# Mixer 1's head steps and attention in closer, later steps, a convolution tap on ScalarE, and smaller edits in mixer 2 and at the end

## Chip, core and metric

One core of a Trainium2 chip runs the whole program. The metric is the device time of one execution in microseconds, the median of several; lower is better.

## What is computed

A batch of one, 256 tokens, 1024 channels, all in float32. Two blocks follow each other. The part that matters here is the first block's hybrid mixer and what lies around it:

```python
proj = h @ w_in                      # c_q, c_kv, k_rope, conv_in (3 x 512), gate_logits (2 x 1024)
q = rms_norm(c_q) @ w_uq             # 8 heads, 64 + 32 (rope)
kv = rms_norm(c_kv) @ w_ukv          # 8 heads, 64 + 64
# q and k: rms norm per head, rope on the 32; causal softmax attention -> o_attn
u = gate_c * xv
u = conv1d(u, conv_w, kernel=3, causal, per channel)
o_conv = gate_b * u
merged = sum(sigmoid(gate_logits) * (branches @ w_branch))
y = merged @ w_out
```

Before it stands a SwiGLU FFN (width 2816), behind it another; the second block has two attentions (A: 8 heads of 128, B: dilated groups with a bias), gates, an MLP of 4096, a gated embedding, and a last RMS norm over the 1024 channels of each token, whose result is stored.

## The kernel before

Activations lie channels by tokens. Weights stream from HBM in units of 128 x 2048 float32 (1 MB; 16 tiles of 128 x 128), in the order of `unit_list`, into four raw buffers. ScalarE casts each unit to a rounded high part (`hi`, two halves of 1024 columns), VectorE makes the low part, raw minus high (`lo`, per half), into a ring of four. A tile is then three matmuls, high by high, high by low and low by high, over 256 token columns or 258: the last two hold the modulation's shift through the same weights, which is read out of the bank as one column. `ada` units in the same stream are the modulation's matrices; VectorE reduces them against silu(c).

`Plan` writes one list of steps; each engine's program runs its own steps of the list in that order, so the list fixes every queue. A counter of tiles paces the work beside the matmuls: `need` takes units up to three ahead, `fill` and every fourth tile (`PACE`) emit one pending piece (an `ada` or a `lo` half) where more than two are pending, `in_tiles` runs a function so many tiles later, and a side generator is advanced each time that the tile count passes a multiple of `every`.

Mixer 1, after the query and key products, counts tiles from 0: conv_out 0 is 0 to 16, conv_in 2 to 32, conv_in 3 to 48, conv_out 2 to 64, then eight blocks of gates to 192 (order 1, 2, 0, 3 to 7). Each block has two banks of a ring of four, freed when both VectorE's product with the token factor (`rbc`) and ScalarE's copy of the shift column are through. `heads(t)` (`heads_q`, `heads_rope`; VectorE) norms and rotates the queries of 128 tokens at tiles 17 and 20. `head_keys` (`heads_k` on VectorE, `heads_kr` on ScalarE) is at tile 34. The attention starts at tile 42, a step at each multiple of `STEP_1` = 7 of the whole count: eight head turns (four for queries, four for keys; TensorE transposes, ScalarE copies out), then eleven steps of `in_steps`. In step n these emit `normal_1(n-1)`, `scores_1(n)` with `masked_1` and `exp_1`, `turn_1(n-2)` with its copy `turned_1`, and `pv_1` of the pair that ends with n-3 with `o_hi_1`, `o_lo_1`. The first turn falls on tile 54, the first scores on tile 110, the last step on tile 180. The turned probabilities have one bank, the scores two.

`conv` (VectorE) takes conv_in's two products to u, then three taps: one tensor_scalar and two scalar_tensor_tensor. `gate_tanh` follows this chain for each half of a gates block: ScalarE's `gate_shift`, VectorE's `gate_in`, which waits for the shift, a halving of the shift by ScalarE, the tanh.

In mixer 2 attention B has steps of `STEP_B` = 12 tiles beside the 128 tiles of gate_a and out_a; what is left is emitted behind them at once (`finish_side`). At the end the second token half's result is scaled by ScalarE (columns 0 to 511) and VectorE (512 to 1023) and stored in one transfer of 512 KB.

## Time and profile before

| | us |
|---|---|
| median of 3 runs | 1015.24 (1014.84 to 1017.86) |
| the profiled execution | 1014.84 |
| its span, first to last instruction | 1013.1 |
| TensorE busy | 983.3 |
| VectorE busy | 776.2 |
| ScalarE busy | 536.2 |

By stage the span divides into a start to 18 us, the first FFN to about 217, mixer 1 to about 385, the second FFN to 594, mixer 2 to 765, the MLP to about 975 and the end. A timeline row is start, length, engine, line, operation, out<-in, count, and in brackets the idle time before it and what ended it. Helpers record all operations, so lines say little and tiles (sb_ring are weights, sb_tq and sb_tmp temporaries, sb_zb the shift columns, sb_junk<-sb_raw an ada piece, R the big shared region) say more. PEclk is the granted TensorE clock, 1.00 for the higher of its two levels.

### The profile page before, as it was taken

The numbers are of one execution on the slowest core, as the hardware profiler recorded it, in microseconds if no ns is written. First come the engines' busy times: TensorE is split into PE (matmuls) and PEld (weight loads), VectorE is DVE, ScalarE is ACT, GpSimd is POOL, SyncE is SP. The second block draws the span as 40 slices with busy tenths as digits, with TensorE's granted clock in tenths as the row PEclk, the third lists the DMA queues.
The fourth block names the chain that finished last, engine by engine and source line by source line (L and its number), as shares of the span: only waits on it lengthen the run. The fifth ranks groups of instructions, "written<-read, shape, count | busy, mean of one in ns | idle before, by whom it ended". The sixth has DMA issues, their size and how long they took to land.

```text
span 1013.1 us, 17325 instructions
## 1 busy us (share of the span) xinstructions
PE 983.3 (97%) x7016; PEld 917.8 (91%) x7016; DVE 776.2 (77%) x1423; ACT 536.2 (53%) x937; POOL 12.5 (1%) x32
## 2 busy tenths in 40 slices
PE   5999999999898999999999999999999999999996
PEld 4999998999897999999998988789999988988895
DVE  6999998979976887685776588556778877577665
ACT  5455554436576555453555545664555655355453
POOL 0000000004000000000000000000000000000000
PEclk9999999999999999999999999999999999999999
DMA  8996999855572655678664535364454555555531
GB/s 334 352 345 268 350 344 341 298 205 209 177 276 93 213 200 174 240 240 209 246 241 174 191 135 208 125 182 136 141 186 168 196 173 203 196 178 173 181 105 41
DMA packets 33277, 213.92 MB, mean 211 GB/s; under 512 B 3757, under 2 KB 6189, under 8 KB 8494
## 3 DMA queue, kind: packets, MB, share of 16 engines
q1 hardware_dynamic: 32910, 211.78, 59.5%
q8 instruction: 55, 0.90, 0.3%
q10 hardware_dynamic: 288, 1.05, 0.3%
q14 instruction: 24, 0.20, 0.1%
HBM read 210.19 MB, written 2.62 MB: 210 GB/s over the span
## 4 chain that ended last, share of the span: by engine, by line
PE 89%; DVE 6%; ACT 3%; issue 1%; DMA 1%; DVEq 0%; ACTq 0%
PE bank L216 87%; PE bank L219 2%; DVE sb_ring L195 1%; ACT sb_tmp L192 1%; ACT sb_ring L192 1%; ACT R L192 1%; DVE sb_tq L195 1%; DVE sb_tmp L195 1%; DVE sb_junk L204 1%; DMA sb_raw<-wts 0%; DMA sb_x<-xt 0%; DVE sb_acc L195 0%; DVE sb_st_v L207 0%; DVE sb_tmp L198 0%; DVE sb_nst L195 0%
## 5 line engine op out<-in xcount | busy, mean ns | idle before, releaser
L216 PE MATMUL bank<-sb_h,sb_ring 128*128 128x258 f32 (+2 forms) x3776 | 496.4, 292 | 6.7 <-DVE sb_h L201 3.9
L216 PEld LDWEIGHTS bank<-sb_h,sb_ring 128*128 128x128 f32 x3776 | 475.7, 190 | 20.9 <-issue 5.7
L195 DVE TENSOR_TENSOR sb_ring<-sb_raw,sb_ring 128x1024 fp32r<-128x1024 f32 (+1 forms) x324 | 385.2, 1205 | 2.8 <-ACT sb_ring L192 2.8
L192 ACT ACTIVATE sb_ring<-sb_raw 128x1024 fp32r<-128x1024 f32 (+1 forms) x324 | 320.4, 1038 | 79.3 <-DMA sb_raw<-wts 47.1
L216 PE MATMUL bank<-R_512r,sb_ring 128*128 128x256 f32 (+1 forms) x1608 | 225.3, 301 | 0.0
L216 PEld LDWEIGHTS bank<-R_512r,sb_ring 128*128 128x128 f32 x1608 | 211.3, 188 | 11.9 <-issue 0.3
L216 PE MATMUL bank<-sb_ring,sb_h 128*128 128x512 f32 (+1 forms) x504 | 112.5, 378 | 0.0
L216 PEld LDWEIGHTS bank<-sb_ring,sb_h 128*128 128x128 f32 x504 | 87.4, 188 | 16.6
L204 DVE CUSTOM_DVE_ANT_0 sb_junk<-sb_raw,sb_csil,sb_cols 128x1024 bf16<-128x1024 f32 x72 | 92.3, 1282 | 1.8
L216 PE MATMUL bank<-R_1024r,sb_ring 128*128 128x512 f32 (+1 forms) x576 | 91.6, 320 | 0.0
L216 PEld LDWEIGHTS bank<-R_1024r,sb_ring 128*128 128x128 f32 x576 | 82.0, 188 | 8.2
L195 DVE TENSOR_TENSOR sb_tq<-bank,sb_rbc 128x256 f32<-128x256 f32 x87 | 34.6, 421 | 62.5 <-ACT sb_zb L192 40.3
L192 ACT ACTIVATE R_512r<-sb_tq 128x256 fp32r<-128x256 f32 x60 | 25.2, 420 | 77.1 <-DVE sb_tq L195 50.1
L192 ACT ACTIVATE sb_tmp<-bank 128x256 f32<-128x256 f32 (+2 forms) x62 | 27.9, 462 | 30.0 <-PE bank L216 27.7
L192 ACT ACTIVATE sb_tmp<-sb_tmp,sb_smx 128x256 f32<-128x256 f32 (+2 forms) x40 | 21.0, 526 | 34.8 <-DVE sb_smx L204 24.5
L201 DVE SCALAR_TENSOR_TENSOR sb_x<-bank,sb_gcol,sb_x 128x256 f32<-128x256 f32 x36 | 17.4, 482 | 27.5 <-PE bank L216 27.1
L192 ACT ACTIVATE sb_h<-sb_x,sb_cols 128x256 fp32r<-128x256 f32 x24 | 14.2, 592 | 37.5 <-DVE sb_x L201 24.0
L195 DVE TENSOR_TENSOR R_512r<-sb_tq,R_512r 128x256 fp32r<-128x256 f32 x60 | 25.2, 420 | 3.9 <-ACT R_512r L192 3.9
L192 ACT ACTIVATE sb_tq<-bank 128x256 f32<-128x256 f32 (+1 forms) x35 | 12.9, 368 | 27.1 <-PE bank L216 27.0
L195 DVE TENSOR_TENSOR sb_tmp<-bank,sb_tmp 128x256 f32<-128x256 f32 x32 | 12.4, 425 | 19.0 <-ACT sb_tmp L192 19.0
L219 PE MATMUL bank<-sb_con,sb_tmp 128*128 128x128 f32 (+1 forms) x134 | 21.2, 276 | 6.0 <-ACT sb_tmp L192 4.2
L192 ACT ACTIVATE sb_tq<-sb_tq,sb_zb 128x256 f32<-128x256 f32 x26 | 13.3, 511 | 23.7 <-DVE sb_tq L195 23.6
(158 smaller groups left out, 558.1 us busy)
## 6 DMA issues: line engine op xcount, KB each, us to landing
sb_raw<-wts SPq DMA_DIRECT2D x193, 1024.0 KB, 4.9
sb_raw<-wts SPq DMA_DIRECT2D x3, 512.0 KB, 3.9
scratch<-R SPq DMA_DIRECT2D x1, 1536.0 KB
sb_x<-xt ACTq DMA_DIRECT2D x2, 512.0 KB, 5.2
out<-R SPq DMA_DIRECT2D x2, 512.0 KB, 2.6
R<-scratch SPq DMA_DIRECT2D x2, 508.0 KB, 8.9
sb_raw<-wts SPq DMA_DIRECT2D x1, 768.0 KB, 4.5
sb_raw<-wts SPq DMA_DIRECT2D x1, 640.0 KB, 4.0
```

What stands on the lines that cost most here:

```text
L192: return Issued(self.e and self.e.activation(o, i, func, **kw))
L195: return Issued(self.e and self.e.tensor_tensor(*a))
L201: return Issued(self.e and self.e.scalar_tensor_tensor(*a))
L204: return Issued(self.e and self.e.tensor_tensor_reduce(*a))
L216: return Issued(self.e and self.e.matmul(o, w, m, start=start, stop=stop, skip_group_check=True))
L219: return Issued(self.e and self.e.transpose(o, i, ident))
```

## The change

Times of steps in mixer 1: `HEADS_AT` (17, 20) to (37, 53), `KEYS_AT` 34 to 75, `ATTENTION_AT` 42 to 70, and the generator is advanced each 3.5 tiles instead of 7. A head turn takes one such half step; a step of the attention takes two (`in_half_steps`): scores, turn and pv in the first, the norm of the scores just made and the copy-out of the last pv in the second. By the tile count the turns fall on tiles 75, 79, 82, 86 (queries), 89, 93, 96, 100 (keys), the scores on 103, 110 and so on, their norms on 107, 114 and so on, the last first-half step on 173.

While that generator's stretch lasts (`apart`), the cast of a unit is emitted in two places: its first half when the unit is taken, its second just ahead of the unit's first `lo`.

In the convolution the tap of a token itself is one ScalarE pass (`conv_tap`), between `conv_u` and the other two taps, with one more `fill` there. In gates, VectorE's `gate_in` of both halves comes first and waits for the matmuls alone; ScalarE's `gate_shift` halves in the same pass and frees the bank; the separate halving is gone. `exp_ready` is a one-element exp after the first FFN's up blocks. `STEP_B` is 10.5. The last result is scaled in quarters of 256 columns and stored as two transfers (each two runs of 256 columns per token).

```diff
-STEP_1, STEP_A, STEP_B = 7, 11, 12
-HEADS_AT, KEYS_AT, ATTENTION_AT = (17, 20), 34, 42
+STEP_1, STEP_A, STEP_B = 7, 11, 10.5
+HEADS_AT, KEYS_AT, ATTENTION_AT = (37, 53), 75, 70
...
-            self.add("hi", i, w)
+            self.add("hi", i, w, (0,) if self.apart else (0, 1))
+            if self.apart:
+                self.late.add(w)
...
+            if name == "lo" and a[0] in self.late:
+                self.late.remove(a[0])
+                self.add("hi", i, a[0], (1,))
             self.add(name, i, *a)
...
+        self.add("exp_ready")
         self.add("gcol", 0, 0.5)
...
             self.fill()
-            self.add("conv", i, xs, zc, y)
+            self.add("conv_u", i, xs, zc, y)
+            self.add("conv_tap", i, y)
+            self.fill()
+            self.add("conv", i, y)
...
             banks = project(("gates", f), [128, 128], between)
+            qs = [tq.take() for _ in banks]
             for i, b in enumerate(banks):
-                zb, q = m.zb.take(), tq.take()
+                self.add("gate_in", f, i, b, qs[i])
+            for i, b in enumerate(banks):
+                zb, q = m.zb.take(), qs[i]
                 self.add("gate_shift", f, i, b, zb)
-                self.add("gate_in", f, i, b, q)
-                done(b, ("gate_in", f, i))
+                done(b, ("gate_shift", f, i))
                 self.add("gate_tanh", f, i, q, zb)
...
-                    self.add("o_hi_1", h // 2, o)
+                    o_b.append((h // 2, o))
+
+            def between(n):
+                if n < 8:
+                    self.add("normal_1", n, p_b[n])
+                if o_b:
+                    hp, o = o_b.pop()
+                    self.add("o_hi_1", hp, o)
                     self.fill()
-                    self.add("o_lo_1", h // 2, o)
-                    done(o, ("o_1", h // 2))
-
-            yield from in_steps(scores, lambda h: self.add("normal_1", h, p_b[h]), turn, pv)
+                    self.add("o_lo_1", hp, o)
+                    done(o, ("o_1", hp))
+
+            o_b = []
+            yield from in_half_steps(scores, turn, pv, between)
 
         def start():
-            self.side, self.every = attention(), STEP_1
+            self.side, self.every, self.apart = attention(), STEP_1 / 2, True
...
         self.finish_side()
+        self.apart = False
...
         self.add("final_factor", 1)
-        self.add("final", 1)
-        self.add("store", 1)
+        for half in range(2):
+            self.add("last_final", half)
+            self.add("last_store", half)
...
+def in_half_steps(scores, turn, pv, between):
+
+    for n in range(11):
+        yield
+        for i, stage in ((0, scores), (2, turn), (3, pv)):
+            if 0 <= n - i < 8:
+                stage(n - i)
+        yield
+        between(n)
...
+        e.dma_start(quarters(m.out[1, :, :], half), quarters(m.result(1), half)).then_inc(
+            *self.up(f"out{1 + half}_out", ("out", 1 + half), by=16))
...
+    def conv_tap(self, i, y):
+
+        e = self.e
+        e.wait_ge(*self.at("conv_u", i))
+        e.wait_ge(*self.at("cols"))
+        e.activation(y.ap[:, 0:T], y.ap[:, T:2 * T], scale=self.m.cc("conv", 8 + i)).then_inc(
+            *self.up("conv_tap", ("conv_tap", i)))
...
+        e.activation(m.smx[0:1, 0, 7:8], m.ones[0:1, 0:1], FN.Exp).then_inc(*self.up("scalar_own"))
...
-        e.wait_ge(*self.at("project", ("gates", f)))
-        e.activation(zb.ap[:, 0:1], bank.ap[:, T:T + 1]).then_inc(*self.up("shift_out", ("gate_shift", f, i)))
+        e.wait_ge(*self.at("gate_in", f, i))
+        e.activation(zb.ap[:, 0:1], bank.ap[:, T:T + 1], scale=0.5).then_inc(*self.up("shift_out", ("gate_shift", f, i)))
...
-        e.activation(zb.ap[:, 1:2], zb.ap[:, 0:1], scale=0.5).then_inc(*self.up("scalar_own"))
-        e.wait_ge(*self.last())
-        e.wait_ge(*self.at("gate_in", f, i))
...
-        e.wait_ge(*self.at("gate_shift", f, i))
+        e.wait_ge(*self.at("project", ("gates", f)))
         e.tensor_tensor(q.ap, bank.ap[:, 0:T], m.rbc, ALU.mult).then_inc(*self.up("gate_in", ("gate_in", f, i)))
```

## Rows read from the trace of the kernel before

**Rows 1.** The page's first part and two of its costliest groups (busy, instructions; mean ns)
```profile
PE 983.3 (97%) x7016; PEld 917.8 (91%) x7016; DVE 776.2 (77%) x1423; ACT 536.2 (53%) x937; POOL 12.5 (1%) x32
...
L195 DVE TENSOR_TENSOR sb_ring<-sb_raw,sb_ring 128x1024 fp32r<-128x1024 f32 (+1 forms) x324 | 385.2, 1205 | 2.8 <-ACT sb_ring L192 2.8
L192 ACT ACTIVATE sb_ring<-sb_raw 128x1024 fp32r<-128x1024 f32 (+1 forms) x324 | 320.4, 1038 | 79.3 <-DMA sb_raw<-wts 47.1
```

**Rows 2.** Windows by stage: length, busy us (count) by engine, PEclk, DMA, GB/s
```profile
240.00:262.00 22.00, 19.42 (x152) 18.63 (x150) 21.41 (x53) 11.03 (x20) 7.41 (x19) 1.00 0.55 192
262.00:285.00 23.00, 22.83 (x176) 22.50 (x177) 22.02 (x36) 16.01 (x33) 0.00 (x0) 0.93 0.58 194
285.00:330.00 45.00, 39.85 (x315) 36.99 (x314) 30.54 (x87) 30.91 (x85) 0.00 (x0) 1.00 0.45 165
```

**Rows 3.** The same view in steps of 10 us, the one with a lower clock
```profile
260.00:270.00 10.00, 7.83 (x51) 7.65 (x52) 9.79 (x20) 5.31 (x12) 0.00 (x0) 0.83 0.23 67
```

**Rows 4.** TensorE's timeline in mixer 1: start, us, instructions, idle before
```profile
254.15 5.67 PE L216 MATMUL bank<-sb_h,sb_ring 128*128 128x258 f32 x45 [0.40 <-ACT sb_zb L192]
262.17 4.12 PE L216 MATMUL bank<-sb_h,sb_ring 128*128 128x258 f32 x18 [2.35 <-ACT sb_zb L192]
266.13 0.60 PE L219 MATMUL bank<-sb_con,R 128*96 128x128 f32 x4
...
269.11 0.60 PE L219 MATMUL bank<-sb_con,R 128*96 128x128 f32 x4
...
298.42 0.55 PE L219 MATMUL bank<-sb_con,sb_tmp 128*128 128x128 f32 x3 [1.20 <-DVE sb_tmp L198]
...
308.37 0.55 PE L219 MATMUL bank<-sb_con,sb_tmp 128*128 128x128 f32 x3 [1.81 <-ACT sb_tmp L192]
```

**Rows 5.** VectorE's timeline in mixer 1, forms apart
```profile
237.08 0.35 DVE L198 TENSOR_SCALAR sb_tmp<-sb_tmp,sb_cols 128x256 f32<-128x256 f32 x1
...
256.83 0.69 DVE L195 TENSOR_TENSOR R<-R,sb_st_z 128x512 f32<-128x512 f32 x1
...
261.43 0.42 DVE L195 TENSOR_TENSOR sb_tq<-bank,sb_rbc 128x256 f32<-128x256 f32 x1
...
265.05 1.29 DVE L195 TENSOR_TENSOR R<-R,sb_st_z 128x512 f32<-128x512 f32 x2
...
270.10 1.00 DVE L201 SCALAR_TENSOR_TENSOR sb_tmp<-sb_tmp,sb_cols 128x255 f32<-128x255 f32 x2
...
279.08 0.42 DVE L195 TENSOR_TENSOR sb_tq<-bank,sb_rbc 128x256 f32<-128x256 f32 x1
```

**Rows 6.** ScalarE's timeline, end of the first FFN and mixer 1
```profile
148.80 2.01 ACT L192 ACTIVATE sb_ring<-sb_raw 128x1024 fp32r<-128x1024 f32 x2 [0.85 <-DMA sb_raw<-wts]
...
262.15 0.51 ACT L192 ACTIVATE sb_tq<-sb_tq,sb_zb 128x256 f32<-128x256 f32 x1
...
292.52 1.28 ACT L192 ACT_TABLE_LOAD   x1 [2.35 <-DVE sb_smx L204]
...
294.89 0.20 ACT L192 ACTIVATE sb_zb<-sb_zb 128x1 f32<-128x1 f32 x1
```

**Rows 7.** TensorE's timeline, end of attention B
```profile
739.74 0.60 PE L219 MATMUL bank<-sb_con,sb_tmp 128*128 128x128 f32 x4
741.52 1.09 PE L216 MATMUL bank<-sb_tmp,R 128*64 128x128 f32 x16 [1.18 <-ACT sb_tmp L192]
```

**Rows 8.** SyncE's timeline before attention B
```profile
683.58 1.24 SPq L222 DMA_DIRECT2D R<-scratch  x2
```

**Rows 9.** DMA issues by line: KB each, median us to landing
```profile
out<-R SPq DMA_DIRECT2D x2, 512.0 KB, 2.6
...
R<-scratch SPq DMA_DIRECT2D x2, 258.0 KB, 5.6
```

**Rows 10.** Timeline of the last 17 us, VectorE's last instruction
```profile
1009.15 0.75 DVE L201 SCALAR_TENSOR_TENSOR R<-R,sb_nst,R 128x512 f32<-128x512 f32 x1
```

**Rows 11.** Windows at the end
```profile
1011.00:1011.50 0.50, 0.00 (x0) 0.00 (x0) 0.00 (x0) 0.00 (x0) 0.00 (x0) 0.50 0.99 410
```

More of the change, by code:

```diff
@@ L425, in p_pair, with quarters @@
         return self.reg(34, 512, F32R), self.reg(36, 512, F32R)
+def quarters(ap, half):
+    return ap.rearrange("p (a s n) -> p a s n", a=2, s=2)[:, :, half, :]
 def by_head(ap):
@@ L473, in __init__ @@
         self.pend, self.split, self.hold = [], set(), False
+        self.apart, self.late = False, set()
         self.tiles, self.side, self.every, self.later = 0, None, 4, []
@@ L1330, in run @@
                  "bias_store": self.bias_store, "load_bias": self.load_bias, "load_p": self.load_p,
-                 "store": self.store, "end": self.end}
+                 "store": self.store, "last_store": self.last_store, "end": self.end}
         for name, args in self.plan.steps:
@@ L1410, in load_p, with store, last_store @@
             *self.up("gain_in", ("fin_row",), by=16))
-    def store(self, i):
+    def store(self):
         m, e = self.m, self.e
-        e.wait_ge(*self.at("final_low", i))
-        if i:
-            e.wait_ge(*self.at("final_high", i))
-        e.dma_start(m.out[i, :, :], m.result(i)).then_inc(*self.up(f"out{i}_out", ("out", i), by=16))
+        e.wait_ge(*self.at("final"))
+        e.dma_start(m.out[0, :, :], m.result(0)).then_inc(*self.up("out0_out", ("out", 0), by=16))
+    def last_store(self, half):
+        m, e = self.m, self.e
+        e.wait_ge(*self.at("final_low", half))
+        e.wait_ge(*self.at("final_high", half))
+        e.dma_start(quarters(m.out[1, :, :], half), quarters(m.result(1), half)).then_inc(
+            *self.up(f"out{1 + half}_out", ("out", 1 + half), by=16))
     def end(self):
         e = self.e
-        e.wait_ge(*self.at("out", 0))
-        e.wait_ge(*self.at("out", 1))
+        for i in range(3):
+            e.wait_ge(*self.at("out", i))
         e.wait_ge(*self.at("scratch"))
@@ L1906, in run, with hi @@
                 steps[name](*args)
-    def hi(self, i, w):
+    def hi(self, i, w, parts):
         m, e = self.m, self.e
@@ L1912, in hi @@
             e.wait_ge(*self.at("used", w - NS))
-        for p in range(2):
+        for p in parts:
             a, b = m.half(w, p)
@@ L2629, in conv_c, with conv_u @@
         e.tensor_tensor(y.ap[:, T:2 * T], bank.ap[:, 0:T], m.rbc, ALU.mult).then_inc(*self.up("conv_c", ("conv_c", i)))
-    def conv(self, i, xs, zc, y):
-        m, e = self.m, self.e
-        u, yy = y.ap[:, T:2 * T], y.ap[:, 0:T]
-        w = [m.cc("conv", 4 * n + i) for n in range(3)]
+    def conv_u(self, i, xs, zc, y):
+        e = self.e
+        u = y.ap[:, T:2 * T]
         e.wait_ge(*self.at("conv_xs", i))
@@ L2638, in conv @@
             *self.up("conv_u", ("conv_u", i)))
-        e.wait_ge(*self.last())
-        self.ts(yy, u, w[2], ALU.mult)
+    def conv(self, i, y):
+        m, e = self.m, self.e
+        u, yy = y.ap[:, T:2 * T], y.ap[:, 0:T]
+        w = [m.cc("conv", 4 * n + i) for n in range(2)]
+        e.wait_ge(*self.at("conv_tap", i))
         for n in (1, 2):
-            e.wait_ge(*self.last())
+            if n == 2:
+                e.wait_ge(*self.last())
             e.scalar_tensor_tensor(yy[:, n:T], u[:, 0:T - n], w[2 - n], yy[:, n:T], ALU.mult, ALU.add).then_inc(
```

52 lines of the change are left out of this document (29 added, 23 removed).

## Prediction

> **What bounds the kernel now.** I read the page's first part, then the windows of the three engines by stage, then TensorE's timeline in every stretch that is not full, and for each gap there the timelines of VectorE and ScalarE. TensorE is busy 983.3 us of a span of 1013.1 [rows 1]. It starts late and ends early by about 20 us together; the gaps between hold under 10 us. They lie where the change works. From 240 to 262 us TensorE misses 2.58 us while VectorE is busy 21.41 of 22; from 262 to 285 VectorE is still busy 22.02 of 23 and TensorE nearly full; from 285 to 330 TensorE misses 5.15 us while no engine is full [rows 2]. So the first is a VectorE backlog, the last a chain of short waits. One gap costs twice: between 260 and 270 the granted clock is 0.83 of full [rows 3], which is 3.4 us at the lower level (1.2 GHz) and 1.7 us of matmul work lost, right behind the longest wait of the mixer, 2.35 us. The matmuls show it: 18 of them take 4.12 us there [rows 4], where the prices below give 2.2. In mixer 2, TensorE waits 1.18 us in the last step of attention B, which falls behind the tiles that should cover it [rows 7].
>
> Prices I use throughout: seven tiles (21 matmuls) and one head turn repeat every 2.98 us (266.13 to 269.11) [rows 4]; I split this as 0.365 us a tile and 0.42 a turn, which also fits 45 matmuls in 5.67 us [rows 4].
>
> **Part 1, heads and keys later.** The 2.35 us wait is for a bank that conv_in 2 holds; its VectorE product runs at 261.43, and just ahead of it stand both heads' query steps, 256.83 to 261.43, 4.60 us [rows 5]. TensorE had conv_in 2 behind it just before 254.15 [rows 4], so VectorE lagged by 8 us. Moved to tiles 37 and 53, the heads leave that place. The four tensor_scalar taps also leave VectorE, 0.35 us each, 0.39 with the gap to the next [rows 5]; two of them (0.78 us) stand before this point. So conv_in 2 is read at 261.43 - 4.60 - 0.78 = 256.05, and TensorE wants the bank at 259.4: the 2.35 us go, and the 1.7 us of slow clock with them. The 0.40 us wait at 254.15 [rows 4] hangs on a shift copy behind VectorE's convolution gate, which comes 0.78 earlier: it goes too. Gain 0.40 + 2.35 + 1.70 = 4.45 us.
>
> The work is moved, not removed, so I follow VectorE's queue. In the plan the extra fill in each conv_in takes one weight half (1.2 us [rows 1]) earlier and the pacing then takes one fewer: counting pending halves block by block gives the same number ahead of every tile multiple of 16. heads(0) then ends near 262.8; conv_in 3 is read by 263.5, wanted at 265.2 (tile 64 is 259.4 + 16 x 0.365). heads(1), before the gates of conv_out 2, ends at 271.0 (end of conv_in 3's convolution in before, 270.10 + 1.00 [rows 5]) less the 1.2 of heads_k (row at 265.05), less 1.56 for four taps, plus 1.13 for the weight half now ahead of it: 269.4. The first query turn is at tile 75, TensorE's 269.3. **New wait 0.1 to 0.3.** heads_k, at tile 75, comes behind everything that stood before gates 1's first product at 279.08 [rows 5], less four taps: done at 277.5. The first key turn is at tile 89: 269.3 + 0.2 + 14 x 0.365 + 4 x 0.42 = 276.3. **New wait 1.2 us**, bounds 0 (a weight half slips behind it) and 2.6 (one more slips ahead; the clock stays up, as it did through 1.81 us [rows 2, 4]). I take 1.5 for both. Behind the waiting turn TensorE holds the tiles of gates 0; VectorE and ScalarE gain on it meanwhile. Banks: gates 1's are free near 278.7, wanted at 281: covered.
>
> The taps on ScalarE: the nearest row is a 128x256 pass with a per-partition operand, 0.51 us [rows 6]. ScalarE must wait for conv_u first, with a cast queued behind it (up to 1.6 us later for conv_in 2). In the trace the halves that VectorE takes next were cast some 4 us before; nothing reaches TensorE. Bounds 0 and 0.5; I take 0.
>
> **Part 2, first attention, 5.15 us of gaps.** Three causes show. (a) The first exp loads its table, 1.28 us at 292.52 [rows 6], with VectorE's next product behind it; the first gap, 1.20 us before turn(0) at 298.42 [rows 4], follows. exp_ready puts the load behind the first FFN's last silu, where ScalarE idles 0.85 us for a transfer until 148.80 [rows 6]: the load delays that cast by some 0.45 us, for weights that are three units away. Cost 0; with the cover gone it would be 1.28 on a cast that still has that lead. The tanh of the gates run behind this exp without another load, so it holds. (b) In each gates block VectorE's product waits for ScalarE's shift, and ScalarE passes a second tiny copy (0.20 [rows 6]): two round trips of 1.2 us in order. Now VectorE reads at once, and ScalarE has two shifts and two tanh without a wait between the engines: some 1 us less on it per block. (c) A weight cast holds ScalarE for 2.0 us in one piece, two halves of 1.04 [rows 1]; 1.81 us of gap at 308.37 [rows 4] end on a copy out of the turn bank that stood behind casts. Apart, it blocks 1.04. Besides, normal(n) comes three tiles (1.1 us) earlier against turn(n). The start is one step earlier (scores at tile 103 instead of 110), the period of seven tiles stays, and the last step is at tile 173 of 192. The window from 285 to 330 holds some ten steps: (45 - 5.15)/10 = 3.98 us of TensorE each, and 3.1 of ScalarE and 3.05 of VectorE [rows 2]. At 78% on both, in an order that alternates between them, some waits stay. Gain between 3.0 and 5.15; I take 5.15 - 0.6, plus 0.3 for six restarts of the array, whose first group takes longer (estimated at 0.05 each): 4.85 us.
>
> **Part 3, second attention.** Steps of 12 tiles start at tile 12 of 128; the eleventh lands behind tile 128, where turn(7) (739.74) and the product that waits for its copy stand together [rows 7]. In steps of 10.5 it lands at tile 125. Gain 1.2. It starts 4 tiles (1.5 us) earlier, near 690; the bias rows it needs are issued at 683.58 and 684.4 [rows 8] and such a transfer lands after 5.6 us [rows 9], at 690: at worst VectorE waits 0.5 there, with one weight half behind it. Bounds 0.6 and 1.2; I take 1.2.
>
> **Part 4, the end.** The last 512-column operation of VectorE (0.75 us from 1009.15 [rows 10]; ScalarE has its like beside it) becomes two of about 0.45 (256 columns take 0.42 [rows 5]), so the first half's store is issued 0.3 us earlier, the second at the old time with half the bytes. The old store lands 2.6 us after issue [rows 9], of which 512 KB at the 410 GB/s of its own time [rows 11] are 1.25. Half the bytes: 0.6 less at most, but both halves share the engines and rows of 1 KB are less efficient. Bounds -0.5 and +0.4; I take -0.2. The Trainium skill speaks on both sides here ("Perfetto Trace Analysis", DMA Optimizations): pieces under 2 KB carry "significant per-transfer overhead", and splitting lets some start sooner when the engines are idle. "DMA: Bandwidth & Descriptors" (its fit under the two cost components) has 2.0 us plus bytes at 436 GB/s, by which the last piece would end 0.6 us sooner, an estimate; the trace has 2.6 for 512 KB where the fit gives 3.2, so it already disagrees by as much.
>
> **Sum**, against the profiled execution (1014.84 us, 1.7 outside its span): -4.45 + 1.5 - 4.85 - 1.2 - 0.2 = -9.2, so 1005.6. The median run lies 0.4 above the profiled one: **1006.0 us**.
>
> **Rivals.**
> A, the debt comes back: heads and keys are now so late that turns wait longer than 2 us and the clock falls again as it did at 262. Price: waits of 3 instead of 1.5, and 1.7 for the clock: +3.2, 1009.2. For it: VectorE is busy 22.02 of 23 there, and my margins are 1 to 2 us. Against: moved items keep their place among known neighbours, and a shorter gap of 1.81 us left the clock alone.
> B, the attention is bound by the single turn bank and ScalarE's load of 78%: only 2.5 of 5.15 go. +2.4, 1008.4.
> C, all waits go and no new one comes: -1.5 and -0.6 more, 1003.9.
> D, slower: the second half of each cast now stands in ScalarE's queue just ahead of its lo piece, behind exps that wait for VectorE; VectorE then waits in order and TensorE runs out of weights. Seven units are taken while apart is on. It decides from 9.2/7 = 1.3 us of stall a unit; at 2 us a unit it is +4.8 net, 1020. Against: about 4 us between cast and use in the trace, and three units of lead.
> E, the early load does not help because a load stands at the first exp anyway: +1.2, 1007.2, inside the main range.
>
> **How the numbers follow.** Forecast with E 0.60, A 0.15, B 0.13, C 0.09, D 0.03. The range 1002.8 to 1010.0 takes in A, B, C and the bounds (new waits 0 to 3, attention 3.0 to 5.15, end -0.5 to +0.4). About 0.3% (3 us) is what a measurement of this kernel can tell from no change; faster by more: the forecast, B, C and nearly all of A, 0.92; same 0.05; slower 0.03.
>
> **What would show it.** Right: no 2.35 us gap ahead of conv_out 2 and granted clock 1.00 through 260 to 300; heads_k ending within 1 us of the first key turn, with a short gap there; no table load between 280 and 300, one near 148; under 1 us of gaps in the attention; no gap at attention B's last product. Wrong: a slow-clock stretch near 270 to 280 (A); gaps ahead of turn groups at each cast (B); TensorE waiting for VectorE's sb_ring (D).

## The result

The changed kernel takes 1011.21 us (median of 5 runs, 1010.49 to 1012.35), the kernel before 1017.16 beside it (5 runs, 1014.84 to 1017.98): ratio 0.9948, 95% interval 0.9937 to 0.9959. It is faster by about half a per cent. Forecast were 1006.0 us and a range that ends at 1010.0, so the time lies above the range; faster by over 0.3% (0.92) held. The two profiled executions, 1014.84 and 1011.21 (span 1009.4), differ by 3.6 us where the working had 9.2.

Page after (busy time of the engines; the group of VectorE's weight pieces), to be read with [rows 1]. TensorE's work is the same, and VectorE's pieces now wait 10.3 us for ScalarE's casts instead of 2.8:

```profile
PE 982.6 (97%) x7016; PEld 917.6 (91%) x7016; DVE 774.3 (77%) x1420; ACT 535.0 (53%) x927; POOL 11.8 (1%) x32
...
L195 DVE TENSOR_TENSOR sb_ring<-sb_raw,sb_ring 128x1024 fp32r<-128x1024 f32 (+1 forms) x324 | 385.6, 1205 | 10.4 <-ACT sb_ring L192 10.3
```

Windows after (busy of PE, PEld, DVE, ACT, POOL, then PEclk), to be read with [rows 2, 3]:

```profile
240.00:262.00 22.00, 22.00 (x175) 21.48 (x174) 21.11 (x48) 14.83 (x26) 7.47 (x22) 1.00 0.55 197
...
262.00:285.00 23.00, 19.89 (x154) 19.37 (x154) 21.26 (x40) 12.58 (x25) 0.00 (x0) 0.93 0.60 217
...
285.00:330.00 45.00, 43.35 (x348) 40.51 (x347) 32.37 (x90) 28.95 (x77) 0.00 (x0) 1.00 0.46 165
...
270.00:280.00 10.00, 7.02 (x45) 6.79 (x46) 9.96 (x18) 6.12 (x15) 0.00 (x0) 0.83 0.57 206
```

The first window is full now, but the second lost what it gained: TensorE misses 3.11 us there, and the granted clock of 0.83 moved from 260 to 270 into 270 to 280. The attention misses 1.65 instead of 5.15. TensorE's timeline after, every row of mixer 1 with a new or changed gap, then the start of the branch matmuls and the gate group behind attention B ([rows 4, 7] before):

```profile
235.53 6.79 PE L216 MATMUL bank<-sb_ring,R_512r 128*128 128x512 f32 x34 [1.12 <-ACT sb_tq L192]
...
270.03 0.53 PE L219 MATMUL bank<-sb_con,R 128*96 128x128 f32 x3 [0.15 <-DVE R L195]
...
276.48 1.09 PE L219 MATMUL bank<-sb_con,R 128*96 128x128 f32 x4 [2.96 <-ACT R L192]
...
299.21 0.55 PE L219 MATMUL bank<-sb_con,sb_tmp 128*128 128x128 f32 x3 [0.26 <-ACT sb_tmp L192]
...
319.85 0.55 PE L219 MATMUL bank<-sb_con,sb_tmp 128*128 128x128 f32 x3 [1.39 <-ACT sb_tmp L192]
...
334.46 5.80 PE L216 MATMUL bank<-R_512r,sb_ring 128*128 128x256 f32 x47
...
738.74 3.02 PE L216 MATMUL bank<-sb_h,sb_ring 128*128 128x256 f32 x24
```

The ledger against the kernel before, from the starts of like groups in both timelines (the branch is the first of the branch matmuls behind mixer 1's gates): queries 234.49 to 235.53, **1.04 late**; branch 337.71 to 334.46, **3.25 early**; the first group of the next ada unit 574.49 to 571.78, **2.71 early**, so 0.54 is given back in the second FFN; last scaling operation 1009.15 to 1005.25, **3.90 early** (1.2 from attention B); from there to the end 3.95 before and 4.15 after. Sum 3.7.

### The profile page after: what moved, and what is told of

The parts are those of the page before. It is cut to its first block, busy times and chain, and to the rows that moved or that the text cites. A ratio compares the mean times of both kernels' runs of the same rounds, so it can differ in the third digit from the quotient of the medians.

```text
span 1009.4 us, 17305 instructions
## 1 busy us (share of the span) xinstructions
PE 982.6 (97%) x7016; PEld 917.6 (91%) x7016; DVE 774.3 (77%) x1420; ACT 535.0 (53%) x927; POOL 11.8 (1%) x32
## 3 DMA queue, kind: packets, MB, share of 16 engines
q10 hardware_dynamic: 288, 1.05, 0.3%
HBM read 210.19 MB, written 2.62 MB: 211 GB/s over the span
## 4 chain that ended last, share of the span: by engine, by line
PE 80%; DVE 9%; ACT 4%; DMA 4%; issue 2%; SPq 0%; DVEq 0%; ACTq 0%
PE bank L216 78%; DMA sb_raw<-wts 3%; DVE sb_ring L195 2%; ACT sb_ring L192 2%; PE bank L219 2%; ACT sb_tmp L192 1%; DVE sb_junk L204 1%; DVE sb_tq L195 1%; DVE sb_tmp L195 1%; DMA R<-rows 1%; DVE sb_tmp L201 1%; ACT R L192 0%; DMA sb_x<-xt 0%; DVE R_512r L195 0%; DVE sb_tmp L198 0%
## 5 line engine op out<-in xcount | busy, mean ns | idle before, releaser
L195 DVE TENSOR_TENSOR sb_ring<-sb_raw,sb_ring 128x1024 fp32r<-128x1024 f32 (+1 forms) x324 | 385.6, 1205 | 10.4 <-ACT sb_ring L192 10.3
```

Source lines behind the costliest of these rows:

```text
L195: return Issued(self.e and self.e.tensor_tensor(*a))
```

## The experiments

Times are of one profiled execution each, but for the last version's; the kernel before took 1014.95, 1016.49, 1016.53, 1017.04 and 1016.21 beside the five sets. Diffs are against the changed kernel. Executions of one kernel differ by up to 4 us (1007.38 to 1011.39 for the last version), so the argument rests on starts within the traces, not on these times. A single start is not exact either: the two small transposes at 231 us, ahead of what the edits change in mixer 1, start between 230.9 and 231.3 (where the ada unit isn't moved). The time between two events of one trace is free of that.

Three events come back below. The product is VectorE's first pass on the banks of conv_out 0, near 252 us. The turn is the first head turn that waits for VectorE, near 270. The branch is the start of the branch matmuls, near 334.

### The tap by ScalarE

```diff
-self.add("conv_tap", i, y)      # ScalarE
+self.add("conv_tap_v", i, y)    # VectorE, the tensor_scalar of before
```

> The changed kernel with the token's own tap of all four conv_in blocks back on VectorE, in the same place of the order and with the same fills. Theory Q (the tap holds ScalarE's queue: its cast and the copy c_sums_out behind it free the bank that the query products want): the 1.12 us wait of TensorE before the query products (235.5 us) is gone, they start within 0.1 us of the kernel before (234.5), and VectorE's waits of 0.24, 0.17 and 0.47 us between 234 and 241 go too. VectorE then carries 4 x 0.39 us more, so its convolution gate of conv_out 2 comes about 0.7 later than in the changed kernel while TensorE is 1.0 earlier: the wait at the third query turn grows from 2.96 to about 4.7. Rival (the wait before the queries comes from the extra fill, not from the tap): it stays at 1.0 or more.

1011.45. The 1.12 us gap is gone, and the queries start at 234.30. So the tap has a cost where the prediction put none. ScalarE's timeline after shows how:

```profile
232.76 0.51 ACT L192 ACTIVATE sb_tmp<-sb_tmp,sb_cols 128x256 f32<-128x256 f32 x1 [0.63 <-DVE sb_tmp L201]
233.17 1.99 ACT L192 ACTIVATE sb_ring<-sb_raw 128x1024 fp32r<-128x1024 f32 x2
235.07 0.21 ACT L192 ACTIVATE sb_tq<-bank 128x72 f32<-128x72 f32 x1
```

The tap waits 0.63 us for `conv_u`; the cast (2.0 us, 232.12 before) starts 1.05 late, and behind it stands the 0.21 us copy that frees the bank TensorE wants for the queries. But the time did not fall: the gap at the first waiting head turn grew from 0.15 to 1.16 us (270.41), and one of 1.35 came at 281.81. The branch starts at 334.83. The third turn waits 2.95 us as in the changed kernel, where 4.7 was expected, and this time no stretch of half clock follows.

### Moving head steps and the attention's start

```diff
-HEADS_AT, KEYS_AT, ATTENTION_AT = (37, 53), 75, 70
+HEADS_AT, KEYS_AT, ATTENTION_AT = (17, 20), 34, 70    # heads as before
```

> The changed kernel with heads and keys back at tiles 17, 20 and 34; the attention still starts at tile 70 in half steps. Theory D (the heads' 4.6 us of VectorE set when conv_in 2's banks come free): a wait of about 2 us before conv_out 2 returns near 260 us, with 3.4 us of the lower clock behind it. Theory S (the wait at the third query turn is ScalarE's queue held by VectorE's lag, whatever the heads are): the lag is paid at conv_out 2, heads_kr is out of ScalarE's way (0.7), and the wait at the third turn falls from 2.96 to under 1 us. Rival (the heads only have to be done before their turns, VectorE's total does not matter): no wait returns at conv_out 2, and the one at the turn goes; the kernel would be 4 us faster than the changed one.

1011.6. The waits at the first and third turn and the slow stretch behind them are gone; in their place TensorE waits 2.05 us at 262.12, with 3.4 us of half clock behind it, and 1.19 at 281.85:

```profile
262.12 11.72 PE L216 MATMUL bank<-sb_h,sb_ring 128*128 128x258 f32 x81 [2.05 <-ACT sb_zb L192]
```

The branch is at 334.93. **The later heads alone bring 0.5 us at the branch**, where the prediction had 2.55 (2.35 and 1.7 gained, 1.5 lost). Starting the attention 7 or 14 tiles later (`ATTENTION_AT` 77, 84):

> The changed kernel with the attention's start at tile 77 instead of 70: first turn on tile 82, third on 89, scores from 110 as in the kernel before, last step 180. Theory S (ScalarE's copy of the first turn stands behind a whole cast and conv_hi, which wait for VectorE; it ends at 277): TensorE reaches the third turn about 2.9 us later, so the wait of 2.96 us shrinks to under 0.8 and the clock stays at its higher level; the start of the branch products comes 3 to 4.5 us earlier. The whole cast at tile 64 is still whole, and one more at tile 80 is split. Rival (the key turns would wait next, for heads_k, which ends at 278.0): a new wait of 1 us or more at tile 96.

1013.93; the third turn's gap grows to 5.75 us, where under 0.8 was expected.

> The changed kernel with the attention's start at tile 84: first turn on tile 89, scores from 117, last step 187 of 192. Theory S: no wait of over 0.3 us at any turn, clock full from 20 us to the end of the last gates; like the start at 77 or up to 0.8 us better there. Rival (the end of the attention then stands too close to the branch products): the last norms, turns and the copy-out of the last pair end behind tile 192, and TensorE waits at the first branch block, 1 us or more.

1013.81; 4.18 us, where no wait was expected. The branch is at 337.6 both times. The tile count does not decide how long the third turn waits: in both kernels, ScalarE's copies of the first turns stand behind gate steps that wait for VectorE.

### Four banks for the head turns

```diff
+four = [B[0], B[3], B[1], B[7]]
-b = A[hp % 2].take()
+b = four[hp % 4].take()
```

> The changed kernel with the head turns over four PSUM banks instead of two, so that the third turn has a bank without waiting for ScalarE's copy of the first. Theory V: VectorE is the bound, so TensorE runs on by one or two blocks and pays elsewhere: at the first key turn (tile 89), which needs heads_k, done at 278.0 in the changed kernel and wanted at about 276, 1 to 2 us, or at the bank of gates 0; the sum of waits between 260 and 290 stays above 2 us, but as no single wait is over 2.5 the clock may stay up. Theory B2 (the two turn banks are the cause): no wait over 0.5 us between 260 and 290, branch products 4.5 us earlier.

1011.36. The 2.96 us wait is gone, so its cause was the turn bank, which ScalarE read out late. In the changed kernel ScalarE's copies (275.76) stand behind a cast and conv_hi (272.93), and conv_hi waits for VectorE, which is late. VectorE's timeline after has `conv_gated`:

```profile
272.42 0.48 DVE L201 SCALAR_TENSOR_TENSOR sb_tmp<-sb_tmp,sb_zb 128x256 f32<-128x256 f32 x1
```

and ScalarE's timeline of the same kernel:

```profile
272.93 0.42 ACT L192 ACTIVATE R_512r<-sb_tmp 128x256 fp32r<-128x256 f32 x1 [1.39 <-DVE sb_tmp L201]
273.26 1.99 ACT L192 ACTIVATE sb_ring<-sb_raw 128x1024 fp32r<-128x1024 f32 x2
275.15 0.71 ACT L192 ACTIVATE R<-sb_tq 128x256 f32<-128x256 f32 x2
275.76 1.24 ACT L192 ACTIVATE R<-bank,sb_wqk 96x512 f32<-96x512 f32 x2
```

Yet the branch comes later, at 335.18. TensorE now reaches what lies behind sooner, and waits there, by its timeline in this kernel:

```profile
277.70 0.29 PE L219 MATMUL bank<-sb_con,R 128*96 128x128 f32 x1 [0.70 <-ACT R L192]
...
283.11 0.64 PE L219 MATMUL bank<-sb_con,R 128*96 128x128 f32 x4 [1.35 <-ACT R L192]
...
299.42 0.90 PE L219 MATMUL bank<-sb_con,sb_tmp 128*128 128x128 f32 x3 [2.19 <-ACT sb_tmp L192]
```

and ScalarE's timeline of the same kernel:

```profile
281.43 1.06 ACT L192 ACTIVATE sb_ring<-sb_raw 128x1024 fp32r<-128x1024 f32 x1 [1.49 <-DMA sb_raw<-wts]
```

The 1.35 us are a wait for a copy behind this cast, which waits 1.49 us for its weights, a transfer; the changed kernel shows no such wait here.

### The ada unit ahead of conv_in 0, moved to the gates

```diff
-ADA_2 = [0, 4, 4, 4, 13, 14, 15, 19]
+ADA_2 = [0, 4, 4, 13, 14, 15, 16, 19]
```

> The changed kernel with one pair of ada units (two VectorE pieces of 1.25 us) taken out of the place ahead of the query weights and put 12 weight units later, beside the attention; nothing else. Theory V (VectorE's total work up to tile 82 is the bound of this stretch, and every earlier edit only chose where TensorE pays for it): all that VectorE does after 225 us comes 2.5 us earlier, the wait at the third query turn falls from 2.96 to under 1 us, the clock does not fall behind it, and the branch products start 3 to 4.5 us earlier than the 334.5 of the changed kernel. Rival (ScalarE's own order is the bound, its whole cast and conv_hi): the wait stays above 2 us.

1011.57. VectorE idles 2.57 us at 234.08 instead and is 1.3 us earlier from there on, but the third turn waits 2.96 again. In the attention, with two more passes of 1.28 us in it, TensorE waits 3.76. The branch is at 335.39. With four banks:

> Both edits, one ada pair moved and four banks for the turns. Theory V: the debt is gone and nothing holds the turns: waits between 260 and 290 under 0.5 us together, full clock, branch products at 329.5 to 331. Rival (the moved pair makes VectorE late in the attention instead): the waits between 290 and 330 grow from 1.65 to over 3 us.

1010.07, branch 333.66, with a wait of 2.88 us at 297.48 and half clock behind it. The rival's forecast came: 3.86 us of waits in the attention.

### Casts in one piece

```diff
-self.side, self.every, self.apart = attention(), STEP_1 / 2, True
+self.side, self.every, self.apart = attention(), STEP_1 / 2, False
```

> The changed kernel with whole casts during the attention. Theory C1 (my prediction: a whole cast holds ScalarE 2.0 us in one piece and is what the splitting relieves): the waits between 290 and 330 grow from 1.65 to 2.5 or more. Theory C2 (the second half just ahead of its low part now holds VectorE, as 0.72 us before 307.3 and 316.3, with the masks behind it; the wait of 1.39 at 319.9 ends that chain): whole casts shrink the waits to under 1.2 us.

1011.58. The attention's waits are 0.70 and 0.59 (1.29, against 1.65 split), and a wait of 0.77 comes at a key turn, whose copy now stands behind a whole cast (1.99 us from 279.63). The branch is at 334.97. So the split brings 0.5 us at the branch, and it does so at the key turn, not in the attention, where the prediction had its gain. Its cost is seen in VectorE's timeline of the changed kernel: the piece waits for the half cast just ahead of it.

```profile
316.29 1.23 DVE L195 TENSOR_TENSOR sb_ring<-sb_raw,sb_ring 128x1024 fp32r<-128x1024 f32 x1 [0.72 <-ACT sb_ring L192]
```

### Squares on ScalarE: what sets the stretch

Three squares of the heads (1.63 us on VectorE) done by ScalarE:

```diff
-self.add("head_squares", n, t, b, False)
+self.add("head_squares", n, t, b, True)
```

> The changed kernel, with the three squares of the heads' first parts (128x512 and 128x256, 1.63 us in a row on VectorE from 240.75) done by ScalarE, which idles 3.98 us before 252.86. Theory V, VectorE's queue from 240 to 272 sets how long the third query turn waits and what follows: VectorE is 1.6 us less late at 272, the wait of 2.96 us at 276.5 falls to 1.3 to 1.8, no half-clock stretch follows it, the branch matmuls start at 332.0 to 333.2 instead of 334.46, and the execution takes 1008.0 to 1009.8. Theory K, the stretch pays a fixed sum that only moves (as it did when the heads, the tap or the ada pieces were moved): another gap grows by as much, branch at 334.2 to 335.4, execution 1011 to 1012.

1011.53. The first forecast missed; the numbers of theory K hold (branch 335.19), though VectorE did not become less late, which the first took for granted. It has less to do but waits 2.62 us for the squares, which stand behind a cast, so its sums start 0.80 **later** (244.24, after 243.44), 0.2 of which is there at 231 us already. TensorE's timeline from there:

```profile
270.80 0.53 PE L219 MATMUL bank<-sb_con,R 128*96 128x128 f32 x3 [0.44 <-DVE R L195]
...
277.25 0.64 PE L219 MATMUL bank<-sb_con,R 128*96 128x128 f32 x4 [2.95 <-ACT R L192]
...
282.19 0.64 PE L219 MATMUL bank<-sb_con,R 128*96 128x128 f32 x4 [1.35 <-ACT R L192]
...
335.19 6.04 PE L216 MATMUL bank<-R_512r,sb_ring 128*128 128x256 f32 x49
```

The first waiting turn is 0.77 later, the branch 0.73. That is the pattern: what VectorE is late by at the sums comes out at the branch. And the clock is full here from 255 us to the branch, yet the time from turn to branch is 64.39 us, and 64.43 in the changed kernel, where 3.4 us ran at half clock. Three more kernels agree: 64.42 at full clock (all taps on VectorE), 64.43 and 64.40 with the slow stretch (tap split and more on VectorE, both below). The window from 276 to 290, of the changed kernel and of this one:

```profile
276.00:290.00 14.00, 13.52 (x100) 13.39 (x101) 11.04 (x19) 10.00 (x19) 0.00 (x0) 0.88 0.77 287
```

```profile
276.00:290.00 14.00, 11.40 (x94) 11.13 (x95) 11.01 (x18) 10.12 (x22) 0.00 (x0) 1.00 0.80 296
```

TensorE is busy 13.52 of 14 us at clock 0.88 in one, 11.40 at 1.00 in the other, and both pass the next groups after the same time. **The slow clock costs nothing here**: at full clock TensorE waits 1.35 us at 282.19 instead, for a copy by ScalarE that comes no earlier.

The test of the chain adds work: VectorE does two of the squares twice.

```diff
+if n == 0:
+    self.tt(by_head(b.ap[:, 0:8 * w]), src, src, ALU.mult)
 self.tt(by_head(b.ap[:, 0:8 * w]), src, src, ALU.mult, ("head_squares", n, t))
```

> The changed kernel with work added: VectorE does two of the heads' squares (128x512, 0.6 us each) twice, at 240.8. Chain theory: VectorE has no slack from there to the head turns, so the first waiting turn comes 1.1 to 1.3 us later (271.1 to 271.3, its gap 1.3 instead of 0.15), the third turn's wait stays at 2.96, the branch starts at 335.6 to 335.8, and the execution is 1.1 to 1.3 longer. Rival (the wait of 2.96 us at the third turn has slack before it, and it absorbs what comes late): the third turn's wait shrinks by 1.1 and the branch stays within 0.3 of 334.5.

VectorE's timeline of this kernel:

```profile
253.91 0.75 DVE L195 TENSOR_TENSOR sb_tmp<-bank,sb_rbc 128x256 f32<-128x256 f32 x2
```

and TensorE's timeline of the same kernel:

```profile
271.58 0.53 PE L219 MATMUL bank<-sb_con,R 128*96 128x128 f32 x3 [0.41 <-DVE R L195]
...
278.03 0.64 PE L219 MATMUL bank<-sb_con,R 128*96 128x128 f32 x4 [2.96 <-ACT R L192]
...
335.98 6.28 PE L216 MATMUL bank<-R_512r,sb_ring 128*128 128x256 f32 x51
```

VectorE is 1.56 late at the product, the turn 1.55, the branch 1.52. That is more than the 1.1 to 1.3 expected, since the squares take 3.08 us instead of 1.63, but it passes through whole. The third turn waits 2.96 again and absorbs nothing, so the rival fails. The execution takes 1012.29, 1.08 more; the rest comes back in the second FFN. And the tap split, VectorE for conv_in 1 and 0 and ScalarE for 2 and 3:

> The changed kernel with the own-token tap on VectorE for conv_in 1 and 0, on ScalarE for 2 and 3. The chain as read from the runs so far: the first sums of the heads start 0.52 us earlier than in the changed kernel (242.92, as with all taps on VectorE), VectorE's product of conv_out 0 at 251.95 instead of 252.35, the first waiting head turn 17.6 to 17.7 us after it (269.6 to 269.7), and the branch 64.4 us behind that turn: 333.9 to 334.2 with or without a half-clock stretch; execution 1010.4 to 1011.0. Rival (the tap's 1.12 us wait is worth its full price): branch 333.3, execution 1010.0 or less.

The product is at 252.00, the turn at 269.67, the branch at 334.10, all within 0.05 us of where they were expected. The execution took 1011.15, more than the 1011.0 expected; 0.36 us of it are waits for weights at 474.68 and 480.88 (below).

The chain in numbers, us:

| kernel | product | branch | between |
|---|---|---|---|
| before | 252.38 | 337.71 | 85.33 |
| after | 252.35 | 334.46 | 82.11 |
| squares on ScalarE | 253.12 | 335.19 | 82.07 |
| more on VectorE | 253.91 | 335.98 | 82.07 |
| tap split | 252.00 | 334.10 | 82.10 |
| heads early | 252.34 | 334.93 | 82.59 |
| whole casts | 252.23 | 334.97 | 82.74 |
| all taps on VectorE | 251.97 | 334.83 | 82.86 |
| no early table load (below) | 252.35 | 335.68 | 83.33 |
| ada unit moved | 251.03 | 335.39 | 84.36 |

Four kernels agree within 0.04. With all taps on VectorE it is 0.75 more, which is what the two later taps take (2 x 0.39). With the moved ada unit it is 2.25 more, near its two passes (2.56).

### The chain used

Tap split, four banks and the squares together:

> The changed kernel with three edits: the own-token tap on VectorE for conv_in 1 and 0 and on ScalarE for 2 and 3; the head turns through four banks instead of two; the squares on ScalarE as in the run before. Theory V: no 1.12 us gap at the query products (start 234.3), VectorE is 0.8 us later by the two taps and 1.6 less by the squares, so 0.8 less late at 272, the third turn doesn't wait for ScalarE's copy, key turns wait under 0.5, and what is left is the attention, 1.4 to 3 us: branch at 331.0 to 333.0, execution 1006.5 to 1009.0. Theory K: branch at 333.7 to 335, execution 1010 to 1011.5, with a new gap of 2 us or more at the first turns of the attention.

1008.10; product 251.87, branch **331.92**, 80.05 between; branch and time are inside the first forecast. The cast near 279 no longer waits for weights, and the 1.35 us gap is gone. Then the squares put ahead of the cast in ScalarE's order:

> The three edits of the run before the last batch together (own-token tap on VectorE for conv_in 1 and 0, four banks for the head turns, three squares on ScalarE), and the squares are now put into ScalarE's order ahead of the two halves of a cast (2.02 us) that stood before them. Theory C, a chain sets the stretch: query products end, ScalarE's copies out, squares, sums, factors, all VectorE's work of conv_in 2 and 3, t_q(1), head turns, attention. Every us by which the sums start earlier (they started at 242.99, VectorE having waited 1.36 us for ScalarE) comes out at the branch: sums at 241.7 to 242.2, t_q(1) and the branch 0.8 to 1.3 us earlier, branch at 330.6 to 331.1, execution 1006.8 to 1007.4. Rival T: TensorE's own work is by now the bound between 234 and 296 and only the attention waits are left, so the branch moves by under 0.3 (331.6 to 332.0; 1008).

1007.90. This is less than expected and about what the rival allowed. The fourth square still stands behind the cast, and VectorE waits 1.11 us for it: it is 0.31 earlier at the product (251.56), the branch 0.33 (331.59), and 0.10 of both is there at 231 us already. With the ada unit moved:

> The same three edits together with one pair of ada units moved from ahead of conv_in 0 to the gates (places 4, 4, 4, 13, 14, 15 become 4, 4, 13, 14, 15, 16). Theory C: the chain begins at the query products, which start where conv_in 0's weights are ready (one unit less ahead of them), so everything up to the key turns comes 1.0 to 1.7 us earlier, and the ada passes (1.28 us each on VectorE) now stand inside the attention and are paid there if VectorE or ScalarE is full at that place: branch at 330.0 to 331.0 if half or more stays gained, 331.7 or later if it is all paid back.

1009.27, branch 333.09. With whole casts besides:

> All of these edits (tap split, four banks, squares first on ScalarE, ada pair moved) and casts in one piece in the attention. If the half casts cost what the prediction gave them as a gain (their second half stands just ahead of VectorE's piece, which then waits for ScalarE: 10.3 us of such waits after the change against 2.8 before), the attention's waits on TensorE fall by 0.5 to 1.5 us against the split casts. Theory C together with this: branch at 328.5 to 330.0, execution 1004.8 to 1006.3. If both moves are paid back: 331 or later, 1007 or more.

1009.29, branch 332.28. From product to branch the first takes 81.97 us instead of 80.03: most of the two ada passes (2.56) is paid in the attention, and more than moving them freed before it. Whole casts take 81.60, 0.4 less than split ones here, where they took 0.6 more in the changed kernel. So the split has no fixed worth.

### Table load, attention B, the end

Without `exp_ready`:

> The changed kernel without the early load of ScalarE's exp table. The prediction's account (a load at the first exp costs TensorE about its own 1.28 us): a table load of 1.28 us near 294, the first turn of the attention waits 1.0 to 1.6 us instead of 0.26, branch 0.9 to 1.4 later (335.4 to 335.9), execution 1012.1 to 1012.7. Rival (rival E of the prediction: the load is hidden or given back by later waits): branch within 0.4 of 334.46, execution within 0.5 of 1011.2 (on this chip's ratio).

1011.86. The load is back (1.28 us at 290.23), and the first turn of the attention waits 1.48 instead of 0.26:

```profile
300.46 0.55 PE L219 MATMUL bank<-sb_con,sb_tmp 128*128 128x128 f32 x3 [1.48 <-ACT sb_tmp L192]
```

The branch is 1.22 later, but the last scaling only 0.67, since this kernel doesn't lose the 0.54 us in the second FFN. Next, attention B's steps and the second store are undone together and read apart:

```diff
-STEP_1, STEP_A, STEP_B = 7, 11, 10.5
+STEP_1, STEP_A, STEP_B = 7, 11, 12
-e.dma_start(quarters(m.out[1, :, :], half), quarters(m.result(1), half))
+if half: e.dma_start(m.out[1, :, :], m.result(1))
```

> The changed kernel with two late edits undone, read apart in the trace: attention B in steps of 12 tiles instead of 10.5, and the last 512 KB stored by one transfer once both halves of the columns are done (the halved last operations stay). Account of the prediction for attention B: TensorE's gap of 1.18 us comes back near 738 and the stretch from the branch start to the gate that followed it at 742.54 grows by 1.0 to 1.2 us; rival: under 0.4. For the store: if splitting it cost time (the changed kernel takes 4.15 us from the last final factor to the end, the kernel before 3.95), one store gives 3.7 to 4.0; if the halved operations cost it, it stays at 4.1 to 4.4.

TensorE's timeline of this kernel:

```profile
738.90 1.09 PE L216 MATMUL bank<-sb_tmp,R 128*64 128x128 f32 x16 [1.17 <-ACT sb_tmp L192]
```

1012.44. Attention B's gap is back, and from the next ada group to the last scaling it takes 434.67 us, 434.66 before and 433.47 after: its step is worth 1.2 in full. The end takes 4.16 us with one store (span 1010.7 less 1006.54), 4.15 with two. So the second store gains nothing, and the 0.2 us that the end lost go to the halved operations. VectorE takes 0.88 us for both halves against 0.75 [rows 10], and ScalarE, which ends last of the two, 0.91 against 0.72. ScalarE's timeline before, then after:

```profile
1009.15 0.72 ACT L192 ACTIVATE R<-R,sb_nst 128x512 f32<-128x512 f32 x1 [0.80 <-DVE sb_nst L201]
```

```profile
1005.25 0.91 ACT L192 ACTIVATE R<-R,sb_nst 128x256 f32<-128x256 f32 x2 [0.81 <-DVE sb_nst L201]
```

### The version that beats both

Tap split, four banks, squares first, and the end as before (whole operations, one store):

> The version with tap split, four banks for the head turns and squares on ScalarE ahead of the cast (331.59 at the branch, 1007.9 in one look), and the last 1024 columns' scaling in two whole operations and one store, as in the kernel before. Expected: last final factor to end 3.95 us instead of 4.15, branch at 331.5 to 331.9, execution 1007.4 to 1008.0 where the kernel before has 1016.5 to 1017 (ratio 0.9905 to 0.9915), so 3.3 to 4 us under the changed kernel. Rival: the branch's 2.8 us are partly given back behind it (0.5 us were lost at the weight loads near 480 in the changed kernel), ratio 0.992 to 0.993.

Median 1008.64 of 6 runs (1007.38 to 1011.39) against 1016.21 of 11: ratio 0.9932, interval 0.9919 to 0.9945. The profiled execution took 1007.38, with the branch at 331.48 and 3.9 us from the last scaling (1001.70) to the end, as expected. But it is the fastest of the six, and the median lies 1.3 above it, so the ratio missed the 0.9905 to 0.9915 expected. The rival's reason does not hold for the profiled execution: nothing is lost in the second FFN (236.77 us from branch to the next ada group). What lengthens the others stays open. The version beats the kernel before. Against the changed kernel its branch is 3 us earlier, but the two ratios' intervals overlap (0.9937 to 0.9945), so by how much it is faster as a whole isn't shown.

## Why the prediction was wrong

**The sum, 9.2 for 3.7.** To the branch the sum had 7.8 us (4.45 - 1.5 + 4.85), and 3.25 came. Four steps failed, and one assumption lay under them.

1. **"Nothing reaches TensorE; I take 0"** (the tap). It cost a wait of 1.12 us at the queries. I looked at the casts behind the tap and at conv_in 2; what stood behind the cast was the small copy out of the bank that the queries take, and it came just in time before (no gap at 234.49). The "0.78 earlier" of the convolution gate didn't come either: the product just ahead of it is at 252.38 before and 252.35 after. VectorE, two taps lighter, idled 0.24, 0.17 and 0.47 us between 234.5 and 240.8, waiting for matmuls and for ScalarE. The 0.40 us wait at 254.15 went all the same, because TensorE came there a microsecond later.
2. **"New wait 0.1 to 0.3 ... New wait 1.2; I take 1.5 for both."** The first turn waits 0.15, as said. The key turn, for which 1.2 was forecast, has no wait. The wait is at the third turn, 2.96, with the clock's fall behind it. I followed VectorE's queue to the turns and left out ScalarE's, in which the copies of the turns stand behind a conv_hi that waits for the same late VectorE. heads_k ended at 278.0 (predicted 277.5), conv_in 2 was read at 256.81 (256.05): VectorE's queue was well followed.
3. **"I take 5.15 - 0.6."** 1.65 is left. The first gap went from 1.20 to 0.26, and the run without the early load shows 1.22 of it to be that load. The last gap, 1.39, stays. Of the 3.22 us by which the changed kernel is shorter from product to branch, single edits undone price 1.22 (load), 0.75 (two taps), 0.63 (split casts, worth it at the key turn) and 0.48 (later heads). Such prices need not add up, but they leave only 0.14 for the gates' order and the closer steps, which weren't tried apart and from which the prediction took most of this term.
4. **The 1.7 us of clock** counted as a gain. In the changed kernel such a stretch costs nothing, as the full-clock kernels beside it show. What it cost before at 262 wasn't tried alone. With the heads put back it stood there again behind 2.05 us of wait, in place of the 3.11 us of waits and the slow stretch at the turns, and the branch came 0.47 later.

Under all of them lies one reading. I added up TensorE's gaps and took each as time to be had. From 240.75 to 283 VectorE has no idle left (busy 21.11 and 21.26 of the two windows' 22 and 23), and each kernel's gaps there fall where TensorE's own tiles run out ahead of that chain. Taking such a gap away by itself moves it; only shortening the chain (or what ScalarE adds to it, as in the three edits together) brings the branch forward. Outside that stretch a gap was worth its price: 1.22 us for the table load, 1.2 for attention B. I had written that VectorE is busy 22.02 of 23, and used it against rival A's margins only.

**Right**: the table load, at no cost near 148 (rival E is refuted). ScalarE's timeline after:

```profile
147.87 1.28 ACT L192 ACT_TABLE_LOAD   x1
```

and attention B, 1.2 for 1.2 (gap 1.18 before, 1.17 when undone). **The end** was put at 0.2 us gained and lost 0.2, inside its bounds. SyncE issues the two stores one behind the other, so the second can't start when its data is ready. It is issued at 1006.53, 0.4 us after the last operation ends (0.1 in the kernel before), since issuing the first took 0.6. SyncE's queue after has the two in one row:

```profile
1005.81 1.28 SPq L222 DMA_DIRECT2D out<-R  x2
```

By the fit of "DMA: Bandwidth & Descriptors" (the Trainium skill, under the two cost components), 2.0 us plus bytes at 436 GB/s, the last piece would end 0.6 us sooner, an estimate. No run shows that: a store of 256 KB lands 2.5 us after its issue, one of 512 KB 2.6. The page fitted it to transfers issued by gpsimd, and these are issued by SyncE.

**Rivals.** A named the right place (waits of 3 us and a slow stretch at 270 to 280; 3.11 us of waits came), and its time, 1009.2, is nearest. But the 1.7 us that it added for the clock were no cost, and its reason was half of it: the debt came back through ScalarE's queue. That its time is near is partly luck: it counts 1.7 us that cost nothing and leaves out the 1.12 us at the queries. The Trainium skill says ("Perfetto Trace Analysis", Tensor Engine Instruction) that ScalarE and VectorE are strict FIFO; the rows of 272.93 to 275.76 are that rule at work, and a lag on one becomes the other's. D, VectorE waiting for the second half cast, is real in kind: seven waits of 0.53 to 2.67 us, 7.5 in all over seven units, or 1.1 a unit. But no TensorE gap in mixer 1 ends on such a piece, and D's price was for stalls of TensorE (1.3 a unit). B's claim that 2.5 of 5.15 would go was too low; 3.5 went.

**The 0.54 us** of the second FFN are lost near 480 us, where weights come late, by ScalarE's timeline after:

```profile
475.84 2.01 ACT L192 ACTIVATE sb_ring<-sb_raw 128x1024 fp32r<-128x1024 f32 x2 [0.41 <-DMA sb_raw<-wts]
```

and TensorE's timeline of the same kernel:

```profile
480.94 6.25 PE L216 MATMUL bank<-sb_h,sb_ring 128*128 128x258 f32 x50 [0.19 <-DVE sb_ring L195]
```

A cast waits 0.41 us for its weights and TensorE 0.19 for the piece behind. The loss lies there: in the first 140 us behind the branch the changed kernel and the last version both run 1166 matmuls, in the next 10 us 81 against 86, about 0.6 us. Most kernels take 236.8 to 237.0 us from branch to the next ada group. Those with the branch at 334.1 to 335.0 take 237.2 to 237.6, which looks like a matter of when the stretch begins; but the one with whole casts besides, at 332.28, takes 237.6 too. Which transfer comes late, and why, stays open.

## What to carry to other kernels

Before you price a gap, ask whether the engine that ends it has been without idle time for long ahead of it; if so, the gap is where a chain shows, not what it costs, and only work taken off the chain counts. Where no engine is full, as in this kernel's attentions, a gap may be worth its length. When an operation is handed to another engine, follow everything queued behind it there down to the smallest copy that frees a bank, and when steps of one engine are made later, follow the second engine whose in-order queue waits for them. A stretch of slow clock next to waits may be free; compare two kernels from one common event to the next before you count it.

## What the runs showed of the hardware

The granted clock did not go with the length of the gap alone. It fell to its lower level (1.2 GHz) for 3.4 us (granted 0.66 of full from 275 to 280) behind the gap of 2.96 us in the changed kernel. It did so for as long behind 2.35 (before), 2.05 (heads early), 2.59 (ada unit moved with the three edits), 4.18 (start at 84), and 2.88 and 2.19 us (four banks, with and without the moved ada unit), and for 6.8 us behind 5.75 (start at 77). It stayed at the higher one (2.4 GHz) behind 2.95 us (all taps on VectorE), 2.95 (squares on ScalarE), 2.96 (ada unit moved) and 2.06 (start at 84, at 327.67). What decides between them these runs don't tell.

Splitting an operation of 512 columns in two costs 0.13 us more in all on VectorE (0.75 to 0.88) and 0.19 on ScalarE (0.72 to 0.91). ScalarE's table load takes 1.28 us, and the next instruction starts at its end (147.87 to 149.16).
